# A hybrid decoder step on one core: decoding the expert keys by folding in bf16, a new order at the hand-over to the expert loop, and a fifth buffer of v

## The reference

```
s1 = einsum('chk,nk->chn', q[..., :HALF_Q], k1);  s2 = the same with the other half and k2
v1, i1 = lax.top_k(s1, 16);  v2, i2 = lax.top_k(s2, 16)
cand = (v1[..., :, None] + v2[..., None, :])            # 256 sums
sc, ci = lax.top_k(cand, 16)
e1 = take_along_axis(i1, ci // 16);  e2 = take_along_axis(i2, ci % 16)
eid = e1 * 128 + e2;  gate = softmax(sc)
act = gelu(einsum('chkd,cd->chk', exp_u[eid], xc))
out = einsum('chk,chkd->cd', gate * act, exp_v[eid])
```

## Time and profile before

| | |
|---|---|
| median of 3 runs | 1684.84 us (1683.5 to 1684.86) |
| the profiled execution | 1682.85 us |
| its span, first to last instruction | 1681.1 us |
| PE busy | 1604.8 us (95%) |
| DVE busy | 1342.0 us (80%) |
| ACT, POOL busy | 665.3 us, 561.0 us |
| mean granted TensorE clock | 0.986 |
| moved by DMA | 411.59 MB, mean 245 GB/s |

### The profile page before, as it was taken

One profiled execution on the slowest core, in us unless ns is written; L12 is line 12 of the kernel. 1 busy time (PEld: TensorE's weight loads), 2 busy tenths in 40 slices (PEclk: granted clock), 3 DMA queues, 4 the chain that ended last, 5 costly groups with the idle time before them and its releaser, 6 DMA issues.

```text
span 1681.1 us, 25034 instructions
## 1 busy us (share of the span) xinstructions
PE 1604.8 (95%) x8955; PEld 1418.6 (84%) x8955; DVE 1342.0 (80%) x2723; ACT 665.3 (40%) x1088; POOL 561.0 (33%) x539
## 2 busy tenths in 40 slices
PE   7999987999899899969999999999999999999998
PEld 5777665879898899959999999999999999998886
DVE  5788455459999899957888888888888888889886
ACT  5322545333323368843333333333333333333334
POOL 1000000046465600024444445444444444445420
PEclk9999999999999999989999999999999999999999
DMA  8321822143221348888999999999999999999884
GB/s 287 120 73 57 322 76 70 51 143 89 76 76 31 108 132 250 251 297 312 338 333 351 348 339 337 353 348 348 334 346 352 333 337 350 353 336 360 324 314 139
DMA packets 164432, 411.59 MB, mean 245 GB/s; under 512 B 15504, under 2 KB 76462, under 8 KB 162894
## 3 DMA queue, kind: packets, MB, share of 16 engines
q1 hardware_dynamic: 118229, 242.20, 42.6%
q0 software_dynamic: 46080, 167.79, 26.7%
HBM read 375.34 MB, written 33.24 MB: 243 GB/s over the span
## 4 chain that ended last, share of the span: by engine, by line
PE 65%; DVE 10%; POOL 3%; issue 3%; DMA 1%; SPq 1%; ACT 0%; DVEq 0%; POOLq 0%; ACTq 0%
PE bank L1561 31%; PE bank L1513 26%; PE bank L1542 4%; PE bank L1398 3%; POOL hit L1779 2%; DVE ef L2007 1%; PE bank L1448 1%; DMA u<-in_uT 1%; SPq L1340 1%; DVE i L1943 1%; DVE sc L1937 1%; DVE i L1934 1%; DVE placed L2108 1%; DVE ci L1953 1%; DVE cand L1955 1%
## 5 line engine op out<-in xcount | busy, mean ns | idle before, releaser
L1561 PE MATMUL bank<-v_parts,p_high 128*128 128x512 f32 x1404 | 434.2, 390 | 0.7 <-DVE p_low L1913 0.7
L1513 PE MATMUL bank<-h_high,u_high 128*128 128x384 f32 x1024 | 349.5, 341 | 22.1 <-DVE u_low L1913 21.4
L1513 PE MATMUL bank<-h_high,u_low 128*128 128x384 f32 x1024 | 347.0, 339 | 0.0
L1513 PE MATMUL bank<-h_low,u_high 128*128 128x384 f32 x1024 | 346.5, 338 | 0.0
L1827 POOL DMA_INDIRECT rows<-in_u_rows,row_u x160 | 198.4, 1240 | 383.1 <-DVE dots L2141 218.4
L1561 PEld LDWEIGHTS bank<-v_parts,p_high 128*128 128x128 f32 x1404 | 262.1, 188 | 52.6 <-issue 1.8
L1827 POOL DMA_INDIRECT rows<-in_v,row_u x160 | 211.5, 1322 | 241.8 <-DVE y L2151 168.4
L1913 DVE TENSOR_TENSOR u_low<-u,u_high 128x1024 fp32r<-128x1024 f32 x133 | 164.4, 1242 | 155.8 <-ACT u_high L1651 155.5
L1561 PE MATMUL bank<-v_parts,p_low 128*128 128x512 f32 x702 | 275.0, 392 | 0.0
L1513 PEld LDWEIGHTS bank<-h_high,u_high 128*128 128x128 f32 x1024 | 195.1, 191 | 28.4 <-DVE u_low L1913 23.2
L1717 ACT CAST p_high<-gel 128x384 fp32r<-128x384 f32 x128 | 65.9, 515 | 378.7 <-DVE gel L2129 361.6
(11 more groups left out here) (255 smaller groups left out, 2490.4 us busy)
## 6 DMA issues: line engine op xcount, KB each, us to landing
u<-in_uT SPq DMA_DIRECT2D x128, 512.0 KB, 5.5
vv<-in_v SPq DMA_DIRECT2D x117, 512.0 KB, 5.4
gate<-gates_kept SPq DMA_DIRECT2D x30, 768.0 KB, 8.8
gates_kept<-staged SPq DMA_DIRECT2D x11, 2048.0 KB, 9.7
w_in_sb<-in_w_in SPq DMA_DIRECT2D x9, 1024.0 KB, 8.4
wq<-in_w_q SPq DMA_DIRECT2D x16, 512.0 KB, 3.6
ckT<-in_ckT SPq DMA_DIRECT2D x4, 1536.0 KB, 13.2
cv<-in_cv SPq DMA_DIRECT2D x8, 768.0 KB, 11.6
```

The source lines that it names most:

```text
L1513: ins = pe.matmul(a_ps[q % 2][:, 0:DT], x[:, k], y, start=(k == 0 and n == 0), stop=(k == KT - 1 and n == 2))
L1561: ins = pe.matmul(y_ps[2 * (i - 1) + half][:], x[:, b, of], y[:, part], start=(t == 0 and n == 0), stop=(t == NK - 1 and n == 2))
```

## The change

It has six parts.

- **Decode by folding**: instead of one reduction over 16 rows for each half, DVE adds the upper half of the field to the lower three times in bf16, both halves at once, and the last addition writes ef. In the last head the second half's keys are multiplied in by DVE itself, and each half is folded alone.
- **Softmax ahead of the last decoding**, and its loops over tiles made into one instruction.
- **End of the heads**: POOL does the rest of u block 20 (z = 7) ahead of its picks, the keys are transposed ahead of activation 23, the gates behind it; DVE makes the first one-hot fields ahead of the gates' copy.
- **The last block of gates** goes to a tensor of its own, gates_last, as whole partitions, and ACT copies the part that goes to the tile gate. Each later load of gates has two transfers.
- **Next u first**: SP loads block 34 ahead of that store, and its split is at the end of step -1 instead of in step 0.
- **A fifth buffer of v**, v_first, in memory of its own, loaded two blocks of gates ahead of the loop; POOL holds all but two of its first gathers until activation 33 is done.

```diff
-RUN_ON_VECTOR = (0, 1, 2, 7, 8)
+RUN_ON_VECTOR = (0, 1, 2, 8)
-V_BUFS = 4
+V_BUFS = 5
+HELD = 2
 def steps(t):
     if t < 0:
-        return [("u", LEAD), ("w", 0), ("m", 0), ("p", 0), ("a", LEAD - 1)]
+        return [("u", LEAD), ("w", 0), ("m", 0), ("p", 0), ("a", LEAD - 1), ("u", LEAD + 1)]
...
-    if t + LEAD + 1 < NK:
+    if t and t + LEAD + 1 < NK:
         heavy.append(("u", t + LEAD + 1))
...
+        v_first, v_first_parts = over.pair("v_first", "v_first_parts", [P, 2, D])
...
+                if b == NB - 2:
+                    load_v(0)
                 if b == NB - 1:
                     sp.wait_ge(gates_stored[0], all_stored(0))
                     sp.wait_ge(gates_copied[0], 16 * (NB // 2))
-                    for t in range(2):
+                    for t in range(1, 3):
                         load_v(t)
                 sp.wait_ge(g_taken, GB // GT * (b + 1))
...
             def load_gates(g):
                 sp.wait_ge(gated, CG * (g - 1))
-                src = gates_kept[g].rearrange("k b n -> k (b n)")
-                sp.dma_start(gate[:, g % 2].rearrange("k b c t -> k (b c t)"), src).then_inc(gate_in[g % 2], 16)
+                part, of = gate[:, g % 2].rearrange("k b c t -> k b (c t)"), slice(g * CG * GB, (g + 1) * CG * GB)
+                sp.dma_start(part[:, 0:NB - 1], gates_kept[g]).then_inc(gate_in[g % 2], 16)
+                sp.dma_start(part[:, NB - 1], gates_last[:, of]).then_inc(gate_in[g % 2], 16)
...
-            for half in range(2):
-                store_last(half)
+            last = (NB - 1) % 2
             load_u(EARLY + 2)
-            sp.wait_ge(gates_stored[1], all_stored(1))
-            for t in range(2, V_BUFS):
+            sp.dma_start(gates_last, staged[:, last].rearrange("p n t -> p (n t)")).then_inc(gates_stored[last], 16)
+            load_u(EARLY + 3)
+            sp.wait_ge(gates_stored[last], all_stored(last))
+            sp.wait_ge(last_copied, 1)
+            for t in range(3, V_BUFS):
                 load_v(t)
...
                 for q in early_after(n):
-                    if q == WHOLE - 2:
-                        turn_slots()
+                    if q == WHOLE - 1:
+                        turn_slots(0)
+                        turn_slots(1)
                     activate(q)
+            turn_slots(2)
...
+            act.wait_ge(g_taken, DT // GT)
+            nc.scalar.copy(gate[:, :, NB - 1], staged[:, (NB - 1) % 2, 0:2 * CG].rearrange("p (g c) t -> p g c t", c=CG)
+                           ).then_inc(last_copied, 1)
...
+            split_run(2 + TILES)
+
+            pick(PH - 1, 0)
...
             for r in range(ROW_BUFS - 1):
+                if r == HELD:
+                    pool.wait_ge(a_done, EARLY + 2)
                 fetch_row(r)
...
+                for z in range(FOLDS):
+                    w = TOPK * (TOPK >> z + 1)
+                    wait(dve, folded, base + z)
+                    nc.vector.tensor_tensor(part[:, :, :, 0:w], part[:, :, :, 0:w], part[:, :, :, w:2 * w], ALU.add
+                                            ).then_inc(folded, 1)
+                dve.wait_ge(folded, base + FOLDS)
+                nc.vector.tensor_tensor(ef[:, of, 0:m, n], part[:, :, :, 0:TOPK], part[:, :, :, TOPK:2 * TOPK], ALU.add
+                                        ).then_inc(decoded, len(halves))
```

More of the change, by code:

```diff
@@ L1157, in route @@
         over = Region(nc, at, sb.at)
-        vv, v_parts = over.pair("vv", "v_parts", [P, V_BUFS, 2, D])
+        vv, v_parts = over.pair("vv", "v_parts", [P, V_BUFS - 1, 2, D])
         at = sb.at
@@ L1805, in _ @@
                 if n:
-                    pick(n - 1)
+                    for half in range(2):
+                        pick(n - 1, half)
                 for i in range(tiles_of(n)):
@@ L1814, in _ @@
                         split_run(2 + i)
-            pick(PH - 1)
-            for z in range(IN_HEADS[PH - 1]):
-                if z >= 2 + TILES and z not in RUN_ON_VECTOR:
+            split_run(2 + TILES)
+            pick(PH - 1, 0)
+            for z in range(3 + TILES, IN_HEADS[PH - 1]):
+                if z not in RUN_ON_VECTOR:
                     split_run(z)
@@ L2000, in hits, with decode, decode_both @@
                     ins.then_inc(hit_ready, 1)
-            def decode(n):
+            def decode(n, halves):
                 m = tiles_of(n)
-                for half in range(2):
-                    dve.wait_ge(picked, 2 * n + half + 1)
-                    nc.vector.tensor_reduce(ef[:, half, 0:m, n], hit[:, half, 0:m].rearrange("p i k j -> p i j k"), AX_X,
-                                            ALU.add).then_inc(decoded, 1)
+                of = slice(halves[0], halves[-1] + 1)
+                part = hit[:, of, 0:m].rearrange("p h i k j -> p h i (k j)")
+                base = FOLDS * (n if n < PH - 1 or halves[0] else PH)
+                for z in range(FOLDS):
[6 more added lines that the diff above has]
+                                        ).then_inc(decoded, len(halves))
+            def decode_both(n):
+                dve.wait_ge(picked, 2 * n + 2)
+                decode(n, (0, 1))
             def head(n):
@@ L2063, in _ @@
             dve.wait_ge(gate_step, 5)
-            for i in range(4):
-                inv = gsum[:, i].rearrange("p (h o) -> p h o", o=1)
-                ins = nc.vector.tensor_tensor(tops[:, i], tops[:, i], spread(inv, [P, PH, TOPK]), ALU.mult)
-            ins.then_inc(gates, 1)
+            inv = gsum[:, 0:4].rearrange("p i (h o) -> p (i h) o", o=1)
+            nc.vector.tensor_tensor(by_head(tops), by_head(tops), spread(inv, [P, 4 * PH, TOPK]), ALU.mult).then_inc(gates, 1)
             dve.wait_ge(gate_step, 6)
```

107 lines of the change are left out of this document (60 added, 47 removed).

## The result

The changed kernel takes 1667.32 us in the median of 4 runs (1666.36 to 1669.21), the one before 1684.17 in 4 (1681.18 to 1684.86): ratio 0.9908, 95% interval 0.9896 to 0.9919, or 16.9 us. I had said 1658, range 1652 to 1667. The profiled execution of after took 1669.21 us, its span is 1667.6, so against the span of 1681.1 before I have 13.5 us to explain, where the sum said 26.0. This execution is the slowest of the four of after; in the medians the gain is 16.9.

A forecast was written before the change was run, and what follows sets the result against it. PE was taken to bound the kernel, so time could come only from its waits and what holds it. 12.3 + 14 - 0.3 = 26.0 us gave 1656.9 from the profiled execution, 1658.8 from the median; forecast 1658, range 1652 to 1667.

The forecast's parts named there:

- the sum: Whole kernel: 12.3 us up to the gates plus 14 at the loop's head less 0.3 at the tail, 26.0 us saved.
- Heads, 6.5 us: Heads: folding saves DVE 2.5 us a head, so PE's waits go and the last keys come 6.5 us sooner.
- End of the heads, 5.8 us of the first term: Behind the last head: activations 20, 21 and 22 run without a wait, at 4.18 us each, and end at 575.3.
- first term: Heads through gates stage: the fourth hot_b starts at 588.2 instead of 600.5, 12.3 us saved.
- bound of 8: Heads through gates: only 8 us saved if rests of blocks 22 and 23 or the keys are up to 4 us late.
- 576 us: End of the heads: time at which keys and gates are ready, against 580.6 where PE needs them, a cover of 4.6 us.
- Gates transposition and first product: Gates stage: transposition ends at 581.2, first product stands at 583.1, so PE has a new wait of about 1.9 us.
- Head of the loop, 14 us: Loop's start: block 34's wait goes, a new 2 us wait comes before activation 35; 14 us saved, ends 8 and 16.6.
- Steady loop: From 765 to 1530 us PE is always busy: nothing to gain, and a saving ahead moves it as a block.
- Tail: End of the kernel: gates now come by two transfers, which costs 0 to 1 us, taken as 0.3.
- the lock of DVE and POOL: Rival, chance 0.12: two-operand folds and POOL lock each other out, costing 7 us; 19 us saved, 1665.
- The rival of transfers queueing at the loop's head: Part of a 0.24 rival: block 34 or 35 is 6 us late and the clock falls; 20 us saved, 1664.

The follow-up runs named there:

- e1: Changed kernel with block 22's rest made by DVE behind the softmax instead of by POOL behind its picks; 1664.04 us, ratio 0.9889.
- e9: Kernel before with only the change's first part (folds, softmax and end of the heads), head of the loop as before; 1675.36 us, ratio 0.9951.
- e4: Changed kernel with no gather held back at POOL; 1667.58 us, ratio 0.9906.
- e2: Changed kernel with block 35's rounding and rest moved to the front of step 1 of the loop; 1665.73 us, ratio 0.9902.
- e6: Changed kernel with block 35's rest first in step 1 and block 36 asked for ahead of v blocks 3 and 4; 1667.76 us, ratio 0.9913.
- e7: Changed kernel with block 22's rest on DVE, block 35's rest early and block 36 asked for ahead of v 3 and 4; 1665.00 us, ratio 0.9895.
- e15: Changed kernel with block 22's rest on DVE behind the softmax and the reduction instead of the fold in the last head alone; 1663.10 us, ratio 0.9876.
- e3: Changed kernel with the reduction back in place of the folds in all heads and at their end; 1670.69 us, ratio 0.9930.
- e10: Changed kernel with four dots moved from the loop's steps 0 to 2 to steps 100, 105, 110 and 115; 1664.85 us, ratio 0.9900.
- e11: Changed kernel with the same four dots moved to steps 100 to 115 and block 22's rest on DVE; 1662.30 us, ratio 0.9875.

## Why the prediction was wrong, step by step

1667.32 is 0.3 us above the range, less than the runs differ among themselves; that the gain is 16.9 us where 26 was forecast is clear of them. Against the sum's 26.0 the profiled execution has 13.5; the difference of 12.5 falls on these steps. 1.3 of it is the slow variant of activation 22, which three of eight profiled executions with this order have, and 0.6 the late start.

- **Heads, 6.5 us** ("So the whole 6.5 us come back"): 176.93 - 171.86 = 5.1, 1.4 less. Keys stood at 531.45, and head 0 had begun 0.6 later. The four additions of the fold take 1.7 us, as I had said, and 1.97 with their gaps. What I put at nothing is that DVE then meets POOL's picks: 1.7 us in each head of four tiles. Small waits of 0.50 (458.59) and 0.96 us (484.53) stayed. The mechanism was right for head 3, from which the most came: the wait behind head 4's keys fell from 3.74 to 0.50.
- **End of the heads, 5.8 us of the first term: the step that failed.** "Activations 20, 21 and 22 at 4.18 each end at 575.3" took block 22's rest as on time. The change had put it on POOL behind five picks, and I never laid POOL's queue out. Picks from 566.1, 4.4 us long by the 8.9 us that ten of them took before, and a rest of 2.4 would have been done at 572.9, and PE wanted it at 573.3; in fact the picks took 7.75 beside DVE's two-operand work. Ahead of activation 22 came 2.91 us of waiting, and the activation itself took about 3.1 longer at the lower clock; 0.7 us is left of 5.8 (2.1 in the fast variant). e1 moved that one rest and got 3.2 to 4.6 us back here. My bound of 8 for the first term did not cover it either: the fourth hot_b gives 5.1, and 7.1 at best (e9). The keys, "576 us", stood at 579.7, for the same collisions, hidden here by the late block 22.
- **Gates transposition and first product**: the new wait of 1.9 us came out as 1.91, and the gates' stage then ran in step with DVE. The fourth hot_b stood at 595.4 instead of 588.2: this shift is the two points above and the late start.
- **Head of the loop, 14 us**: 722.44 to 758.36 is 35.9 us, before it was 773.69 - 727.58 = 46.1, so 10.2. Block 34 was in time, with nothing to spare, and the queue of 11.4 us on DVE took 12.0 (rest of 34 done at 735.1, that of 35 at 747.07). The term was mis-sized: I gave the new wait 2 and a fallen clock 0.6, and they took 3.40 and 2.95. "What is held at POOL is queued only for dots, which have the time" held (e4). Unseen was what e2, e6 and e7 showed: behind block 35 stands block 36, and behind that v block 3, each late by about as much. My list of what the head moves was also short by one block: it is 13 pieces of 0.52 MB, 6.8 MB and not 6.3, so 18.6 us at 366 GB/s and not 17.
- **Steady loop**: "a saving ahead of it moves it as a block" missed 1.9 us. I took the fifth buffer as free; its address made 18 matmuls of every fifth weighing slower.
- **Tail**: 0.3 counted, nothing seen. The start of head 0, 0.6 us late, belongs to no step.

1.4 + 5.1 + 3.8 + 1.9 + 0.6 - 0.3 = 12.5.

Of the rivals the lock of DVE and POOL comes nearest: it named the place, the sign and 1665. The Trainium skill (SBUF — State Buffer, SBUF: two separate sides) says that a Vector instruction with two SBUF inputs and a GpSimd one that reads SBUF shut each other out for a whole instruction. The trace agrees: the addition of 0.24 us that took 2.27 ended as a POOL instruction ended. I gave this 0.12, since I priced two meetings, where DVE meets POOL's picks in every head, and in the last one over and over. The rival of transfers queueing at the loop's head came true beside it. The time ended just above my range, which had let only one of them go wrong.

Open: what fills the queue in which block 36 takes 12 us, and what decides, in a head of four tiles, whether POOL's first pick waits for DVE (3.48 us) or the picks get in between. The comparisons and picks are the same and begin 0.97 us apart in both; only the decoding ahead of them differs.

## What to carry to other kernels

Where work moves to another engine's queue, lay out that queue item by item too, with the durations it has beside its neighbour and not those it has alone; here one rest behind five picks took back 3.2 to 4.6 of 12 us. When a stall is removed at a place where the DMA engines are full, ask what is late next, and allow for every new wait twice, as stall and as a slow clock that can follow it. Before a transfer is asked for earlier, look whether its buffer is free by then. Cut the span at fixed marks before two executions are compared, and look at a buffer's address when the same instruction has two durations.

## What the runs showed of the hardware

- A matmul that streams 512 columns from a buffer at byte 167136 of each partition (224 modulo 256) took 395 ns in the trace, from 167264 or 167520 390, like those from the old buffers: 4.20 against 4.12 us for 18.
- A reduction of 1280 elements with one operand ran beside POOL's picks and rest in e15, and neither was held up: 2.67 and 2.60 us (2.50 to 2.60 in head 3, with POOL idle), picks at 0.62, the rest 2.40. Additions of two operands and POOL's multiplications held each other up in the same place of after (2.27 us for one of 0.24).
- The same eight comparisons, two rests and eight picks had two courses: DVE 4.0 us and POOL 7.54 (e3, head 1), or DVE 5.7 and POOL 6.92 (after, head 1).
- The 2 MB store of the last gates took 10.62 us to land in after and 12.08 in e10, although its rows are whole partitions; the store of the block before it, in smaller pieces, took 9.32 in after. The traffic beside the two differs, so the worth of larger pieces was not measured.
- Behind waits of 1.9 to 4.6 us ahead of an activation it took 4.43 to 7.27 us, where one without a wait takes 4.35 from its first start to its last end. The same wait had different sequels: of about 2.9 us at activation 22, 6.02 us in e2 and 7.26 in after; of 2.18 us at activation 35, 4.43 us in e10 (granted clock 1.00) and 6.02 in e11 (0.65).
